# Expert rows scattered to fixed rows per token, and a final stage that reads plain rows

## The chip, the core and the metric

The kernel runs on one core of a Trainium2 chip. The metric is the device time of one execution in microseconds, as the median of several runs; lower is better. The engines are named as the profile does: PE (TensorE matmul), PEld (its weight load), DVE (VectorE), ACT (ScalarE), POOL (GpSimd) and SP (SyncE, which only issues DMAs here). A DMA queue belongs to the engine that issues: q1 is SP's, q10 ACT's, and q0 is POOL's, whose descriptors are made in software.

## The reference

One step of a one-layer decoder trunk in float32 for 1024 prompt rows and 32 sample rows, D_MODEL 1024. Token mixers (a state-space branch and a dilated attention branch) come first, then a mixture of 32 experts: each token takes one of four groups and two experts in it. The part around the change:

```
gsel  = argmax(group logits);  w_top, e_top = top_k(softmax(expert logits in the group), 2), normalised
combine[token, expert] = p_group * w_top                      # two nonzeros per token
for e in range(32):
    hid = silu(x @ w_exp_gate[e]) * (x @ w_exp_up[e])         # 1024 -> 256
    out = out + combine[:, e:e+1] * (hid @ w_exp_down[e])     # 256 -> 1024
x = x + gt2 * out                                             # adaLN gate of prompt or sample
y = x * rsqrt(mean(x*x) + 1e-6) * g_final
```

So each of the 1056 tokens has two expert rows of 1024 values. They are added to the token's residual row x2, and the sum is normalised.

## The kernel before, in words

**Stages.** The adaLN vectors and the input projection run to 310 us, then attention with the state-space inputs (to 481 us), the state-space scan, the branch projections, the merge, and from about 820 us one block of code that has the output projection, the router, the expert rounds and the final stage. Every stage is a block with one program per engine; engines meet through semaphores, and the program order within one engine is fixed by hand.

**Attention stage** (lines 880 to 910). POOL is free there but for writing a zero row of the scratch tensor `expert_rows` and the value rows of the outputs. It waits for all of them at the end of the stage.

**Routing.** Token and expert rows are placed in 23 blocks of 128 slots: each expert has 96 slots (the last but one 64), a block is `ROUNDS` index b. VectorE and TensorE work out `slot_i` (the slot of each token's first and second expert), `token_of_slot` (`tok_i`, 4096 for an empty slot) and `weight_of_slot`. Tokens that find their expert full, or that belong to the last expert, go to spare blocks (`token_of_overflow`), at least one, whose number is only known at run time; the loops `Fori(0, turns)` serve them. In the profiled execution there is one turn.

**A round** b (lines 2525 to 2605 for TensorE): POOL gathers the h2 rows of the block's tokens by an indirect DMA, which skips empty slots (line 2345); TensorE turns them (L2529, ACT copies), multiplies with the gate and up weights (L2550, four groups of 32 slots), ACT and DVE make the hidden rows, TensorE turns them (L2559) and multiplies with the down weights (L2572). In TensorE's order iteration b is gate_up(b), turn_x(b+1), down(b-1), turn_hid(b). DVE multiplies both halves of a down product with the token's gate (L3061, L3062) into one of two buffers `y_e`, and ACT stores the buffer to 128 rows of `expert_rows` in slot order (L2714). SP loads the weights of the experts ahead.

**The spare block.** POOL's `loop_block(0)` (L2361 to 2370) stands right behind its last gather; it copies the token numbers and gathers the rows. TensorE turns them (`turn_loop_x(0)`, L2605) after the last round's turn_hid and before `down(ROUNDS - 1)`. Then come gate and up (L2617), the turning (L2621), down (L2629) and the gating into `ly` (L3103).

**The final stage**, inside the loop. POOL stores the last block (L2377) and, per tile of 128 tokens, gathers the first expert's rows (L2385) and gathers the second expert's rows with an add into the same buffer `gr` (L2391). TensorE puts the spare block's rows in token order with a product by a matrix of ones and zeros (L2638), and for five tiles adds `gr` by a product with the identity (L2642). DVE adds the result to x2 (L3119, L3134), ACT squares and sums (L2739, L2741), DVE scales (L3149, L3153) and SP stores (L2324).

Of the kernel before, what the change touches and what calls it, by code (L numbers as in the profile page):

```python
# [14 lines left out]
ALU = mybir.AluOpType  # L15
# [3 lines left out]
I32 = mybir.dt.int32  # L19
# [29 lines left out]
NO_TOKEN, NO_SLOT = 4096, 8192  # L49
# [26 lines left out]
def build(nc, I, O, scratch):  # L76
    ctx = ExitStack()
    with ctx:
# [794 lines left out]
        with ExitStack() as st:  # L873
# [5 lines left out]
            zeros = sb("zero_row", [P, KT], stack=st)  # L879
            g_att = sb("gate_units_att", [P, GB, CW], stack=st)  # L880

            with nc.Block() as block:
                @block.gpsimd
                def _(pool):
# [4 lines left out]
                    pool.dma_start(scratch["expert_rows"][ROUNDS * P:ROUNDS * P + 1, :].rearrange("o (p c) -> p (o c)", p=P),  # L889
                                   zeros[:, :]).then_inc(s_vst, 16)  # L890

                    total = 0
# [17 lines left out]
                    pool.wait_ge(s_vst, 16 * (total + 1))  # L910
# [1210 lines left out]
        tok_i = sb("token_of_slot", [P, ROUNDS], I32)  # L2121
        w_slot = sb("weight_of_slot", [P, ROUNDS])
        tok_ov = sb("token_of_overflow", [P, OVB + 1], I32)
        w_ov = sb("weight_of_overflow", [P, OVB + 1])
        w_top = sb("w_top", [P, 2, NT])
        blk_i = sb("expert_of_block", [1, OVB + 1], I32)
        ids = sb("ids", [P, NT])
# [4 lines left out]
        idx = sb("idx", [P, 1], I32)  # L2132
# [101 lines left out]
        s_lfl, s_rc8 = sem("loop_first_cleared"), sem("x3_root_inverted")  # L2234
        s_lprep, s_lgs = sem("loop_tables_ready"), sem("loop_sample_rows_gated")
        s_lrp, s_lad = sem("loop_rows_of_tile_in_psum"), sem("loop_rows_added")
# [10 lines left out]
        def load_down(sp, e):  # L2247
# [4 lines left out]
        s_gf, s_first, s_both, s_mx, s_sq8, s_m8, s_rt8, s_y8, s_os8 = (  # L2252
            sem("g_final_loaded"), [sem(f"first_rows{t}_gathered") for t in range(NT)], [sem(f"second_rows{t}_added") for t in range(NT)],
            sem("x3_ready"), sem("x3_squares"), sem("x3_mean_square"), sem("x3_root"), sem("y_ready"), sem("y_stored"))
        gr = ([ring_all[:, 4096 + 1024 * t:5120 + 1024 * t] for t in range(4)] + [big[:, 12864 + 1024 * t:13888 + 1024 * t] for t in range(4)]
              + [big[:, 0:1024]])
        loop_gate, loop_at = w_gu_sb[0][:, 0:D], w_gu_sb[0][:, D:D + NT * P].rearrange("p (t n) -> p t n", t=NT)
        tile_first, loop_rel, loop_is = (sb(name, [P, NT]) for name in ("first_of_tile", "loop_token_in_tile", "loop_is_prompt"))
        ADD_ORDER = [TT] + list(range(TT))
        BY_PRODUCT = range(2, 7)  # L2260
# [3 lines left out]
        PAIR = [psum[:, i:i + 2, :] for i in (0, 2, 6, 4)]  # L2264
# [4 lines left out]
        g_row = row_p["gate1"]  # L2269
        def at_of(t):  # L2270
            return slice(TILES.index(t), TILES.index(t) + 1)


        with nc.Block() as block:
            @block.sync
# [917 lines left out]
```

## Time and profile before

| | us |
|---|---|
| median of 3 runs | 1427.6 (1423.43 to 1430.71) |
| span of the profiled execution | 1427.1 |
| own time of the profiled execution beyond its span | not given by the page |
| PE busy | 1343.0 (94%) |
| DVE / ACT / POOL busy | 606.5 / 323.6 / 118.3 |
| mean DMA rate over the span | 171 GB/s |

The span runs from the first to the last instruction of one execution. PE is busy for 94% of it, but this is an average: the last 60 us or so are the final stage, where other engines and the DMA queues work too. The page cuts the span into 40 slices; in the last two PE is busy for 7 and 6 tenths, in all slices of the rounds for 9 or more. Stretches are read from the view of busy time by window, single waits from the instructions in order of time.

### The profile page before, as it was taken

The numbers are of one execution on the slowest core, as the hardware profiler recorded it, in microseconds if no ns is written. First come the engines' busy times: TensorE is split into PE (matmuls) and PEld (weight loads), VectorE is DVE, ScalarE is ACT, GpSimd is POOL, SyncE is SP. The second block draws the span as 40 slices with busy tenths as digits, with TensorE's granted clock in tenths as the row PEclk, the third lists the DMA queues.
The fourth block names the chain that finished last, engine by engine and source line by source line (L and its number), as shares of the span: only waits on it lengthen the run. The fifth ranks groups of instructions, "written<-read, shape, count | busy, mean of one in ns | idle before, by whom it ended". The sixth has DMA issues, their size and how long they took to land. (4 is left out here: it accounts for less than half of the span.)

```text
span 1427.1 us, 21105 instructions
## 1 busy us (share of the span) xinstructions
PE 1343.0 (94%) x8689; PEld 804.0 (56%) x8689; DVE 606.5 (43%) x1290; ACT 323.6 (23%) x692; POOL 118.3 (8%) x135
## 2 busy tenths in 40 slices
PE   4899999999999899999999999999968999999976
PEld 2344448876677666666667666788863333333323
DVE  6743452324342236930752244443663532222247
ACT  4200003545443211123312122111221111110013
POOL 0000001130000060010000000000001000000042
PEclk9999999999999999999999999999968999999997
DMA  9435235330001552332313074620066999999878
GB/s 359 124 96 172 94 99 173 102 96 22 22 28 64 157 171 77 131 90 41 71 53 130 5 246 139 208 96 38 31 245 219 360 376 412 419 416 414 338 250 239
DMA packets 121473, 243.47 MB, mean 171 GB/s; under 512 B 23159, under 2 KB 87303, under 8 KB 112137
## 3 DMA queue, kind: packets, MB, share of 16 engines
q1 hardware_dynamic: 98368, 191.69, 37.7%
q10 hardware_dynamic: 14690, 28.26, 5.3%
q0 software_dynamic: 8320, 22.17, 5.1%
q8 instruction: 69, 1.13, 0.3%
q14 instruction: 26, 0.21, 0.1%
HBM read 208.30 MB, written 37.07 MB: 172 GB/s over the span
## 5 line engine op out<-in xcount | busy, mean ns | idle before, releaser
L2411 PE MATMUL psum<-ring,big 128*128 128x256 f32 x512 | 117.0, 387 | 0.0
L1308 PE MATMUL psum<-h_t,ring 128*128 128x352 f32 x368 | 111.4, 461 | 1.1 <-ACT gate_units L1599 1.1
L2411 PEld LDWEIGHTS psum<-ring,big 128*128 128x128 f32 x512 | 98.4, 195 | 13.9 <-issue 0.4
L2550 PE MATMUL psum<-w_gate_up,u_rows 128*32 128x512 f32 x608 | 101.4, 607 | 2.9 <-DMA w_gate_up<-in_w_exp_up 1.1
L2550 PE MATMUL psum<-ring,u_rows 128*32 128x512 f32 x576 | 101.4, 598 | 0.9 <-ACT u_rows L2699 0.9
L1308 PEld LDWEIGHTS psum<-h_t,ring 128*128 128x128 f32 x368 | 69.0, 190 | 38.3 <-issue 1.6
L2572 PE MATMUL psum<-big 128*32 128x512 f32 x736 | 83.7, 595 | 0.0
L469 PE MATMUL psum<-big,u_rows 128*128 128x512 f32 x144 | 63.9, 593 | 0.0
L2092 PE MATMUL psum<-big,h_t 128*128 128x352 f32 x192 | 60.5, 459 | 1.9 <-PEq L2045 1.9
L2709 ACT ACTIVATE big<-psum 128x256 f32<-128x256 f32 x23 | 8.8, 385 | 231.9 <-PE psum L2550 231.9
L3061 DVE TENSOR_SCALAR v_new<-u_rows,v_new 128x512 f32<-128x512 f32 x46 | 25.1, 546 | 81.4 <-PE psum L2572 80.6
L2550 PE MATMUL psum<-big,u_rows 128*32 128x512 f32 x288 | 56.5, 594 | 1.6 <-DMA w_gate_up<-in_w_exp_up 1.6
L523 PE MATMUL psum<-ring,u_rows 128*128 128x256 f32 x256 | 57.1, 380 | 0.0
L3046 DVE SCALAR_TENSOR_TENSOR big<-big,weight_of_slot,psum 128x256 f32<-128x256 f32 x23 | 11.1, 481 | 107.4 <-ACT big L2709 107.4
L955 PE MATMUL psum<-ring 128*128 128x512 f32 x120 | 55.5, 605 | 0.0
L2550 PEld LDWEIGHTS psum<-w_gate_up,u_rows 128*32 128x32 f32 x608 | 27.0, 112 | 48.1 <-issue 46.5
L791 DVE TENSOR_TENSOR big<-big,psum 128x512 f32<-128x512 f32 x30 | 20.6, 688 | 77.7 <-PE psum L469 77.3
L1069 ACT ACTIVATE p_sb<-s_sb,o_sb 128x128 f32<-128x128 f32 (+1 forms) x96 | 42.0, 439 | 45.4 <-DVE o_sb L1031 45.4
L523 PEld LDWEIGHTS psum<-ring,u_rows 128*128 128x128 f32 x256 | 47.9, 190 | 6.9 <-issue 0.8
L2092 PEld LDWEIGHTS psum<-big,h_t 128*128 128x128 f32 x192 | 36.4, 190 | 22.5 <-issue 2.4
L2550 PEld LDWEIGHTS psum<-ring,u_rows 128*32 128x32 f32 x576 | 26.0, 110 | 40.0 <-issue 38.9
L469 PE MATMUL psum<-h_t,ring 128*128 128x512 f32 x96 | 45.2, 615 | 2.3 <-DVE h_t L756 2.3
(542 smaller groups left out, 2164.6 us busy)
## 6 DMA issues: line engine op xcount, KB each, us to landing
big<-in_w_exp_down SPq DMA_DIRECT2D x32, 1024.0 KB, 10.7
ring<-in_w_ada SPq DMA_DIRECT2D x24, 1024.0 KB, 7.7
w_gate_up<-in_w_exp_gate SPq DMA_DIRECT2D x13, 1024.0 KB, 13.8
w_gate_up<-in_w_exp_up SPq DMA_DIRECT2D x13, 1024.0 KB, 17.1
ring<-in_w_exp_gate SPq DMA_DIRECT2D x13, 1024.0 KB, 10.9
ring<-in_w_exp_up SPq DMA_DIRECT2D x13, 1024.0 KB, 13.2
ring<-in_w_in SPq DMA_DIRECT2D x11, 1024.0 KB, 10.1
h_t<-tmp_gates SPq DMA_DIRECT2D x48, 176.0 KB, 2.6
```

What stands on the lines that cost most here:

```text
L469: m = nc.tensor.matmul(bank_of(g, x), a[:, k, :], h[:, k, :], start=(first and k == 0), stop=(last and k == 3), skip_group_check=True)
L523: m = nc.tensor.matmul(bank[e % NB][:, 0:WB], tokens, w[:, k, :], start=(k == 0), stop=(k == KT - 1))
L791: V.tensor_tensor(out, other, where, ALU.add).then_inc(s_pd, 1)
L955: m = nc.tensor.matmul(bank[7], u_tile[t % 2][:, k, :], w_[:, k], start=(k == 0), stop=(k == KT - 1))
L1069: m = A.activation(p_sb[:, i % 2, s, 0:w], s_sb[:, i % 2, s, 0:w], ACT.Exp, bias=o_sb[:, i % OB, h, HD:HD + 1], scale=1.0, accum_out=o_sb[ ...
L1308: m = T_.matmul(bank[4 + u % 4][:, 0:CW], w_[:, k, c0:c0 + P], ht3[:, k, j * CW:(j + 1) * CW], start=(k == 0), stop=(k == KT - 1))
L2092: m = T_.matmul(bank[b0 + 2][:, 0:CW], w_bs[:, k, m_ * P:(m_ + 1) * P], y2_t[:, k, tok], start=(k == 0), stop=(k == 3))
L2411: m = T_.matmul(bank[2 * (i % 2) + b // 2][0:r, (b % 2) * WB:(b % 2 + 1) * WB], merged_t[:, k, t * P:t * P + r], w[:, k, :], start=(k == 0 ...
L2550: m = T_.matmul(bank[i][at, :], x_t[i][:, k * P + CHUNK * c:k * P + CHUNK * (c + 1)], w_gu[use_of(e, GSLOTS)[0]][:, :, k, :], start=(k == ...
L2572: m = T_.matmul(down_bank(b, f)[at, :], turned(hid_t[b % 2])[:, k, at], w_dn[use_of(e, DSLOTS)[0]][:, k, f * 512:(f + 1) * 512], start=(k ...
L3046: V.scalar_tensor_tensor(out=hid[b % 2], in0=sil[b % 2], scalar=w_slot[:, b:b + 1], in1=bank[b % 2][:, FF:2 * FF], op0=ALU.mult, op1=ALU.m ...
L3061: c.step(dve, V.tensor_scalar(slot_gate, row_p["gate2"][:, at], of_prompt[:, b:b + 1], of_sample[:, b:b + 1], ALU.mult, ALU.add))
```

## The change

- The scratch tensor `expert_rows` gets 4096 rows instead of 2945: row t holds token t's first expert row, row 2048 + t its second, and 128 rows behind token 1055's second one (from 3104) take what belongs to nobody. POOL zeroes rows 0 to 1055 and 2048 to 3231 in the attention stage, by 19 DMAs.
- Every slot now knows its row (`row_of_slot`): an empty one has 6143, which the scatter skips, and the token is the row's low 11 bits.
- POOL, not ACT, writes the expert rows: an indirect scatter per round, behind gather(b) for round b-4; the scatter of round 21 stands ahead of `loop_block(0)`, that of round 22 behind it.
- The spare block's rows are added to their tokens' second rows by an indirect scatter that adds; places without a token add into the rows from 3104. The loop holds only this.
- SP loads the first rows of all tiles with three plain DMAs once all scatters have landed, and the second rows with nine once the adding scatter has landed. DVE, POOL and TensorE add them to x2, in the order FINAL.
- The mean square is taken with the scale and the added epsilon on ACT; the DVE instruction between square and root goes. DVE scales some tiles from PSUM.

The core of the diff:

```diff
-NO_TOKEN, NO_SLOT = 4096, 8192
+TOKENS = 2048
+NO_TOKEN, NO_SLOT = 3 * TOKENS - 1, 8192
+SPILL = TOKENS + N
@@ attention stage, POOL
+cleared = [(a, min(P, end - a)) for start, end in ((0, N), (TOKENS, SPILL + P)) for a in range(start, end, P)]
+for a, r in cleared:
+    pool.dma_start(scratch["expert_rows"][a:a + r, :], zeros[0:r, :]).then_inc(s_vst, 16)
@@ SP, inside the loop, behind the spare block's weight loads
+for i in range(2):
+    sp.wait_ge(s_yst[i], 16 * ((ROUNDS + 1 - i) // 2))
+for i in range(2):
+    sp.dma_start((ring_all[:, 4096:8192] if i == 0 else big[:, 12864:16960]).rearrange("p (t d) -> p t d", t=4),
+                 scratch["expert_rows"][512 * i:512 * (i + 1), :].rearrange("(t p) d -> p t d", p=P)).then_inc(s_fa[i], 16)
+sp.dma_start(gr[TT][0:NS, :], scratch["expert_rows"][SEQ:N, :]).then_inc(s_fa[2], 16)
@@ SP, behind the loop
+sp.wait_ge(s_lst, 16 * turns)
+for t in FINAL:
+    sp.dma_start(gs[t][0:r, :], scratch["expert_rows"][TOKENS + t * P:TOKENS + t * P + r, :]).then_inc(s_fb[t], 16)
+for j, t in enumerate(FINAL):
+    sp.wait_ge(s_y8, j + 1)
+    sp.dma_start(dst, gr[t][0:rows_of(t), :]).then_inc(s_os8, 16)
@@ POOL
+def scatter(b):
+    pool.wait_ge(s_dna, b + 1)
+    pool.wait_ge(s_dnd, b + 1)
+    G.indirect_dma_start(scratch["expert_rows"], bass.IndirectOffsetOnAxis(ap=row_i[:, b:b + 1], axis=0), y_e[b % 2], None,
+                         bounds_check=2 * TOKENS - 1, oob_is_err=False).then_inc(s_yst[b % 2], 16)
 gather(0)
 for b in range(1, ROUNDS):
     if b >= 2:
         pool.wait_ge(s_tx, b - 1)
     gather(b)
+    if b >= 4:
+        scatter(b - 4)
+for b in range(ROUNDS - 4, ROUNDS - 2):
+    scatter(b)
...
-    pool.wait_ge(s_lxg, 16 * (n + 1))
+scatter(ROUNDS - 2)
 loop_block(0, slice(0, 1))
-pool.dma_start(scratch["expert_rows"][P * (ROUNDS - 1):P * ROUNDS, :], y_e[(ROUNDS - 1) % 2]).then_inc(s_lst, 16)
-(18 indirect gathers, first and second rows of nine tiles)
+scatter(ROUNDS - 1)
...
 with pool.Fori(0, turns) as n:
     loop_block(n + 1, bass.ds(n + 1, 1))
+    nc.gpsimd.tensor_copy(l_row[:, :], row_ov[:, bass.ds(n, 1)]).then_inc(s_lrow, 1)
+    pool.wait_ge(s_ly, n + 1)
+    nc.gpsimd.indirect_dma_start(scratch["expert_rows"], bass.IndirectOffsetOnAxis(ap=l_row[:, 0:1], axis=0), ly, None,
+                                 compute_op=ALU.add).then_inc(s_lst, 16)
+    pool.wait_ge(s_lst, 16 * n + 16)
+for t in BY_POOL:                                     # tiles 6 and 7
+    G.tensor_tensor(x2[:, t, :], x2[:, t, :], gr[t], ALU.add).then_inc(s_x2a, 1)
+(sample rows: first rows times gate, added; second rows times gate, added: four operations on 32 partitions)
@@ PE, behind the loop
+for t in (2, 3):
+    start_sum(t, (x2[:, t, :], gr[t]))                # products with the identity into PSUM
+end_sum(2); end_sum(3)                                # the second rows
+for t in BY_POOL:
+    start_sum(t, (x2[:, t, :],))
+end_sum(6); end_sum(7)
@@ DVE
+V.tensor_scalar(tok_i[:, :], row_i[:, :], TOKENS - 1, None, ALU.bitwise_and)
+for t in BY_DVE:                                      # tiles 0, 1, 4, 5: first rows, then second rows in end_add
+    c.step(dve, V.tensor_tensor(x2[:, t, :], x2[:, t, :], gr[t], ALU.add))
@@ the order of the tiles
+FINAL = [0, 2, 1, 3, 4, 6, TT, 5, 7]
```

## Rows read from the trace of the kernel before

**Rows 1.** Stretches: busy us of PE, PEld, DVE, ACT, POOL; then clock, DMA share, GB/s.

```profile
320.00:330.00 10.00, 10.00 (x65) 7.18 (x63) 4.52 (x5) 6.85 (x19) 0.00 (x0) 1.00 0.07 22
1176.00:1200.00 24.00, 24.00 (x216) 8.15 (x212) 6.77 (x12) 2.82 (x4) 1.98 (x2) 1.00 1.02 419
1390.00:1400.00 10.00, 8.40 (x14) 3.71 (x15) 4.39 (x6) 1.35 (x3) 7.46 (x5) 0.68 1.05 286
```

**Rows 2.** What TensorE waited for from 1070 us: engine line, releaser, us, times, longest.

```profile
PE psum L2642 <- DMA ring<-tmp_expert_rows,slot_i: 7.2, 1, 7.2
...
PE psum L2550 <- DMA w_gate_up<-in_w_exp_up: 2.8, 2, 1.6
...
PE psum L2550 <- DMA ring<-in_w_exp_up: 0.6, 1, 0.6
```

**Rows 3.** Instructions of POOL in order of time: start us, us, engine, line, operation.

```profile
311.96 2.17 POOL L905 DMA_DIRECT2D out_pv<-big  x4
...
508.36 3.85 POOL L1289 TENSOR_TENSOR big<-b_bar_c,powers 128x2048 f32<-128x2048 f32 x1 [24.46 <-DVEq L1452]
```

**Rows 4.** VectorE's last instruction before the first gather, same columns.

```profile
1068.33 0.18 DVE L2962 SCALAR_TENSOR_TENSOR token_of_slot<-psum,found_so_far 128x23 int32<-128x23 f32 x1 [0.67 <-PE psum L2472]
```

**Rows 5.** Line 2345, the gathers of the rounds: ns min/median/max, and landing.

```profile
L2345 POOL DMA_INDIRECT big<-tmp_h_rows,token_of_slot x23: 989/992/1143, 1069.5 to 1320.5; - x23
...
DMA to landing us min/median/max: 4.4/8.0/9.5
```

**Rows 6.** The chain of waits in the rounds: start us, us, engine, line, count.

```profile
1077.24 9.59 PE psum L2550 x64
...
1101.35 7.00 PE psum L2550 x64
...
1113.39 7.00 PE psum L2550 x64
```

**Rows 7.** Instructions in order of time, from the spare block's gather to the last round.

```profile
1332.70 0.18 POOL L2363 COPY loop_weight<-weight_of_overflow 128x1 f32<-128x1 f32 x1 [11.21 <-PE psum L2529]
...
1334.01 1.01 POOL L2368 DMA_INDIRECT big<-tmp_h_rows,idx  x1 [0.87 <-POOL idx L2365]
...
1360.08 1.06 PE L2605 MATMUL psum<-ident,big 128*128 128x128 f32 x8
...
1361.07 3.64 PE L2572 MATMUL psum<-big 128*32 128x512 f32 x32
...
1362.50 0.69 DVE L3062 TENSOR_TENSOR big<-psum,v_new 128x512 f32<-128x512 f32 x1
...
1366.72 0.69 DVE L3062 TENSOR_TENSOR u_rows<-psum,v_new 128x512 f32<-128x512 f32 x1
```

**Rows 8.** The chain of waits, where the last round's rows are stored.

```profile
1367.99 2.94 DMA tmp_expert_rows<-u_rows
```

**Rows 9.** Instructions in order of time in the final stage.

```profile
1377.61 1.23 DVE L3103 TENSOR_TENSOR big<-psum,w_gate_up 128x1024 f32<-128x1024 f32 x1 [3.96 <-PE psum L2629]
...
1391.60 3.78 PE L2642 MATMUL psum<-ring,identity_in_first_turn 128*128 128x512 f32 x4 [7.17 <-DMA ring<-tmp_expert_rows,slot_i]
...
1420.78 1.06 ACT L2739 ACTIVATE ring<-h_t 128x1024 f32<-128x1024 f32 x1 [0.99 <-DVE h_t L3134]
...
1422.67 1.28 DVE L3153 SCALAR_TENSOR_TENSOR big<-h_t,ss,u_rows 128x1024 f32<-128x1024 f32 x1
```

**Rows 10.** Line 2391, the gathers that add: landing of its nine DMAs.

```profile
DMA to landing us min/median/max: 4.9/9.7/12.3
```

**Rows 11.** DMA queues from 1371 to 1427 us: packets, MB, share of 16 engines.

```profile
q0 software_dynamic: 2544, 8.65, 62.7%
q1 hardware_dynamic: 1200, 4.33, 19.4%
```

**Rows 12.** The same from 1080 to 1330 us.

```profile
q10 hardware_dynamic: 2609, 9.51, 9.4%
q0 software_dynamic: 3024, 7.46, 8.0%
```

More of the change, by code:

```diff
@@ L2124, in build @@
         w_ov = sb("weight_of_overflow", [P, OVB + 1])
+        row_ov = sb("row_of_overflow", [P, OVB], I32)
+        spill = sb("spill_row", [P, 1])
         w_top = sb("w_top", [P, 2, NT])
         blk_i = sb("expert_of_block", [1, OVB + 1], I32)
-        ids = sb("ids", [P, NT])
+        ids = [sb(f"ids{i}", [P, NT]) for i in range(2)]
         ss5 = sb("ss5", [P, NT])
@@ L2256, in build @@
               + [big[:, 0:1024]])
[L2257 to L2260, printed above, removed]
+        gs = ([w_gu_sb[1][:, 1024 * t:1024 * (t + 1)] for t in range(4)] + [big[:, 4160 + 1024 * t:5184 + 1024 * t] for t in range(2)]
+              + [big[:, 7232 + 1024 * t:8256 + 1024 * t] for t in range(2)] + [big[:, 1024:2048]])
@@ L2396, in _ @@
+                c.step(pool, G.tensor_tensor(gs[TT][0:NS, :], gs[TT][0:NS, :], gate_s, ALU.mult))
+                G.tensor_tensor(x2_s, x2_s, gs[TT][0:NS, :], ALU.add).then_inc(s_x3s, 1)
             @block.tensor
@@ new lines, in _, with end_add, scale @@
+                for t in BY_DVE:
+                    dve.wait_ge(s_fa[A_LOAD[t]], 16 * turns)
+                    c.step(dve, V.tensor_tensor(x2[:, t, :], x2[:, t, :], gr[t], ALU.add))
+                def end_add(j):
+                    t = FINAL[j]
+                    if t in BY_DVE:
+                        dve.wait_ge(s_fb[t], 16)
+                        V.tensor_tensor(x2[:, t, :], x2[:, t, :], gs[t], ALU.add).then_inc(s_x3d, 1)
+                def scale(j):
+                    t = FINAL[j]
+                    r = rows_of(t)
+                    src = PAIR[BY_PE.index(t)] if t in BY_PE else halves(x2_of(t)[0:r, :])
+                    dve.wait_ge(s_rt8, j + 1)
+                    V.reciprocal(ss8[0:r, t:t + 1], ss8[0:r, t:t + 1]).then_inc(s_rc8, 1)
+                    dve.wait_ge(s_rc8, j + 1)
+                    V.scalar_tensor_tensor(out=halves(gr[t][0:r, :]), in0=src, scalar=ss8[0:r, t:t + 1], in1=halves(g_row[0:r, :]),
+                                           op0=ALU.mult, op1=ALU.mult).then_inc(s_y8, 1)
@@ L3162 @@
+                dve.wait_ge(s_gf, 16)
+                for j in range(NT + 1):
+                    if j < NT:
+                        end_add(j)
+                    if j >= 1:
+                        scale(j - 1)
 _OUT = [("y_p", (1, SEQ, D)), ("y_s", (DEC_B, DEC_T, D)),
```

228 lines of the change are left out of this document (89 added, 139 removed).

## The prediction

> **What bounds the kernel now.** Read first the table of busy time by stretch: TensorE is busy throughout every stretch of the attention stage and of the expert rounds, and the DMA engines reach a share of 1.02 and 419 GB/s in the rounds [rows 1]. So a round is held by TensorE, with the transfers just behind it. The list of what TensorE waited for from 1070 us on says how close: weights that came late cost 2.8 us and, by a further row of 0.6 us that stands under it, 3.4 us over 23 rounds; the largest wait of all, 7.2 us, is for rows gathered in the final stage [rows 2]. Then the instructions in order of time around the end of the rounds [rows 7] and in the final stage [rows 9], because the change touches little else. The last round's two halves are written into y_e by 1367.41 us (the second VectorE product starts at 1366.72 and takes 0.69), and the span ends at 1427.1: 59.7 us of tail. There the queues tell what runs: the indirect gathers of q0 move 8.65 MB in 62.7% of 56 us = 35.1 us of all engines (246 GB/s), while the plain stores of q1 move 4.33 MB in 10.9 us (397 GB/s) [rows 11]. The tail is a DMA tail, dear because half of its gathers also add.
>
> **Attention stage.** 19 DMAs of zero rows (9 for rows 0 to 1055, 10 for rows 2048 to 3231) stand in POOL's queue instead of one, 9.2 MB. POOL issues four such DMAs in 2.17 us [rows 3], so 19 take 10.3 us, and its value stores start that much later. At 400 GB/s they hold the DMA engines for 23 us. Beside them TensorE works on what is in SBUF, with the DMA share at 0.07 from 320 to 330 us [rows 1]; the attention rows' stores have four buffers, one per 7 us or so. POOL next has work 160 us later. Cost 0; without that cover it would be at most the 10.3 us. Between 0 and 10.3 I take the near end, since nobody waits there.
>
> **Router.** The second table of ids, epsilon and the spill row are set on VectorE while TensorE merges: 0. The slot map gets a second dependent instruction ahead of the first gather; the existing one takes 0.18 us [rows 4]: +0.2.
>
> **Rounds.** The 22 stores that ACT issued become scatters by POOL. POOL's order is gather(b), then scatter(b-4), which waits for the halves of round b-4. With a period of 12.04 us (1101.35 to 1113.39, [rows 6]; gate and up 7.0, turning 1.1, down 3.6, [rows 6, 7]) gather(b) is issued 0.8 us after the turning of an earlier round; the down product ends 3.6 us later and the two copies 2.6 us after that, so POOL stands in the scatter until some 8 us after the turning and is back 4 us before the next gather. y_e has two buffers, and the scatter has 20 us to land. What changes is bytes: the stores of q10 move every slot and the gathers only slots that hold a token, 9.51 MB against 7.46 MB for about as many rounds [rows 12]; the scatter skips empty slots as the gather does. It costs 20 us of engines for its 7.46 MB (8.0% of 250 us) and replaces 23.5 us. That is 3.5 us off a queue that made TensorE wait 3.4 us. Bounds: -3.4 (all of that wait) and +13 (below, the second rival). I take -2.0.
>
> **The spare block's input.** This is the step that costs. In POOL's order scatter(ROUNDS-2) now stands ahead of loop_block(0), and that scatter waits for the copies of round 21. Before, loop_block(0) ran at 1332.70 and its gather was issued at 1334.01 [rows 7], under cover of two rounds. TensorE's program still turns the gathered rows *before* down(22): turning at 1360.08, down(22) at 1361.07. After: the copies of round 21 end at 1363.19 (1362.50 + 0.69), POOL starts 0.7 later (0.6 from the last copy's end at 1367.41 to the store in [rows 8], and a little for the index) and issues for 0.99 [rows 5]: 1364.9. Three small copies and the gap from 1332.70 to 1334.01 are 1.3 us, with 0.3 for the step between: the gather is issued at 1366.5. It lands after 4.4 (the least of 23, [rows 5]; the median of 8.0 belongs to a full queue; few rows are valid, so below 4.4, to 2.9, is possible as well): 1370.9. TensorE turns at 1371.0 instead of 1360.08: **+10.9**, and everything behind it, down(22), the copies, the spare block's products, goes with it. This wait is new; queued behind it are down(22), the last scatter and both stages of loads.
>
> **The clock.** TensorE has then stood for 9 to 10 us. After a gap of 7.2 us at 1391.60 four products took 3.78 us, and the stretch of 1390 to 1400 has a mean granted clock of 0.68 [rows 9, 1], the two levels being 1.2 and 2.4 GHz. Round 0, after a wait, needs 9.59 for the 64 products that take 7.00 in another round [rows 6]: 2.6. A turning of 1.06 at half speed costs 1.1 more: 3.7. The first turning may count toward what the products need, so I take **+3.0**, bounds 0 and 3.7. By the Trainium skill, "TensorE: Matmul & The Clock Gate", section "Loop structure matters more than you think", a DMA wait of 8 us drops the clock; the trace agrees with its 7.2 us.
>
> **The final stage.** Copies of round 22 end at 1367.4 + 13.9 = 1381.3. The scatter starts 0.6 later; a plain store of the same size landed 2.94 us after issue [rows 8], and I add 1 us for the indirect form: 1385.9. SP then loads the first rows of all tiles, 4.33 MB at 397 GB/s = 10.9 us, landed by 1399. The spare rows are gated at 1378.84 + 13.9 = 1392.7 (the product of 1377.61 lasts 1.23, [rows 9]). POOL's adding scatter starts at 1393.4; a gather that adds landed after 4.9 to 12.3, median 9.7 [rows 10]. Its 0.5 MB goes beside the first loads; I take 7.5, so it has landed at **S = 1400.9**. Only then may SP load the second rows: the first tile's are there at S + 3, the last's at S + 14. The adding of the first rows on VectorE, POOL and TensorE is done beside the waiting. From S + 3: one add 1.23, a square 1.06 [rows 9] with read-out, root and gaps 0.9: the first scaling starts at S + 6.2. Behind it VectorE has nine scalings with their reciprocals at 1.5 (1.28 for the scaling, [rows 9], the rest a guess for the small one) and three more adds at 1.25: S + 23.5. POOL's way is shorter: two adds of 128x1024 at half of the 3.85 of a 128x2048 [rows 3], and four operations on the sample rows at the same 1.93, two of them after their second rows (S + 11.5): S + 15.4, then ACT and VectorE for three tiles: S + 21. The DMA way: second rows until S + 14, stores of 4.33 MB beside the scaling, 10.9 us: S + 25, no later than the last store. For leaving the loop and for VectorE and POOL on each other's feet I add 1: S + 24.5. From the last scaling's end (1422.67 + 1.28) to the span's end it is 3.15 now, and again: S + 27.7 = 1428.5.
>
> The second-rows gathers with their adding, 24 us of engines (35.1 less 10.9), and the products by the placing matrices go; what is late next is the adding scatter, then VectorE.
>
> **Sum** in the profiled execution: rounds -2.0, map +0.2, input and clock +13.9, tail from the end of the copies 47.2 (1428.5 less 1381.3) instead of 59.7, so -12.5; together -0.4: 1426.7. The page gives no time beyond the span of 1427.1, which lies 0.5 under the median 1427.6 of runs from 1423.43 to 1430.71. Adding 0.5: **1427**.
>
> One rule speaks against it. The row of 3.85 us shows POOL's adding with VectorE nearly idle beside it. By the Trainium skill, "SBUF — State Buffer", section "SBUF: two separate sides", a VectorE operation with two SBUF inputs and a GpSimd operation that reads SBUF exclude each other, the later one waiting for all of the earlier. No row of before shows that meeting; it is a rival below.
>
> **Rivals.**
> *The tail is shorter than drawn* (0.25). The adding scatter lands after 4.9 instead of 7.5 (-2.6), the spare rows' gather after 2.9 instead of 4.4 (-1.5), the late weights vanish (-1.4), the clock costs 1 less, 1.5 of VectorE's gaps close: -8, **1419**. For it: few valid rows. Against it: the adding scatter writes all 128 rows, beside full loads.
> *POOL's queue makes gathers late* (0.13, the other side). The gather must land before the next turning, 12.04 - 1.1 - 0.8 = 10.1 us after issue; it lands after 8.0, at most 9.5 [rows 5]. If the scatter ahead of it on the same queue adds over 2.1 us, each of 19 rounds waits for the excess: at 2.8 us 0.7 x 19 = 13, **1440**. Against it: both together are 0.7 MB per round.
> *VectorE and POOL block each other at the end* (0.08): four POOL operations of 1.93 = 7.7 us lie in VectorE's chain: +7, **1434**.
> *The stall is not there* (0.06): TensorE finds the spare rows in time, -13.9, **1413**. The order in POOL's and TensorE's programs speaks against it.
> The forecast has 0.48; its own range is 1421 to 1434. All together, 1415 to 1440. A measurement of this kernel can tell some 0.5% (7 us) from no change, so faster means under 1420.5: 0.30 (two rivals, a little less for the part of the first that stays inside); same 0.49; slower 0.21 (the second rival, most of the third, the forecast's own edge).
>
> **What would show it.** A wait of TensorE of 9 to 11 us before the line that turns the spare block's rows, released by a DMA from the h2 rows; a clock under 1.00 in the 10 us behind it; round periods of 12.04 with waits for weights under 3.4 us in all; 25 to 30 us from the landing of the adding scatter to the end; q0 no longer at 246 GB/s. The forecast is wrong if the wait is under 5 us, if the rounds' gathers are waited for, or if the end follows the adding scatter by over 33 us.

## The result, and the profile after

| | before | after |
|---|---|---|
| median | 1427.54 us (20 runs, 1421.19 to 1434.2) | 1431.69 us (20 runs, 1426.86 to 1440.31) |
| ratio | | 1.0031, 95% interval 1.0016 to 1.0046 |
| span of the profiled execution | 1427.1 | 1429.4 |
| copies of the last round's rows end, to the span's end | 59.7 | 52.5 |

The changed kernel is slower by 0.3%, which 20 runs of each tell from zero. The forecast was 1427 us, no change: the measured median lies 4.7 us above it, inside the forecast's own range of 1421 to 1434, and no slowdown was forecast. The stretches of the two profiled executions say where the difference is. They are cut at instructions that both kernels have: POOL's first zeroing, POOL's first instructions in the next stage and in the router, the first gather, TensorE's start on the last round's turn_hid, and the span's end.

| us | attention | scan to merge | router | rounds | tail |
|---|---|---|---|---|---|
| before | 171.60 | 338.85 | 249.14 | 290.33 | 67.29 |
| after | 173.25 | 338.42 | 245.96 | 288.05 | 72.39 |

The first three columns vary alike in kernels with and without the change: over the fourteen profiled executions of this study (the two kernels and the twelve experiments) attention takes 171.6, 173.25 or 174.7 to 174.9, scan to merge 338.4 to 341.5, the router 245.8 to 246.0, 249.1 to 249.4 or 251.05. The stretch ahead of the table varies as well, from 308.8 to 311.3 (1.4 of the 2.3 us between the two spans lie there). So what the change did is in the last two columns: the rounds gave back 2.3 us and the tail took 5.1. "Tail" is from here on the last column.

**The rounds.** The queues from 1080 to 1330 us of the changed kernel (packets, MB, share of 16 engines), against [rows 12]:

```profile
q1 hardware_dynamic: 14023, 79.13, 79.5%
q0 software_dynamic: 5690, 14.43, 15.1%
```

q10, on which ACT stored 9.51 MB, is no longer in the list, and q0 went from 7.46 to 14.43 MB: 7.0 MB written in place of 9.5.

What TensorE waited for from 1070 us on (engine line, releaser, us, times, longest), against [rows 2]:

```profile
PE psum L2639 <- DMA big<-tmp_h_rows,idx: 13.9, 2, 10.6
PE psum L2563 <- DMA big<-tmp_h_rows,token_of_slot: 3.4, 1, 3.4
PE psum L2677 <- DMA w_gate_up<-tmp_expert_rows: 2.5, 2, 1.9
...
PE psum L2584 <- DMA w_gate_up<-in_w_exp_up: 1.5, 1, 1.5
```

Late weights cost 1.5 us instead of 3.4. The one wait of 3.4 for a round's gather is that of the first round, 3.6 before. At the head of the list is a wait that the kernel before did not have, 10.6 us for the rows of the spare block. (The second of its two times, 3.4 us, is at 1390.38, for the gather of the next spare block, which holds nothing; TensorE then stands again for 1.9 us before the second rows are there, so this one is covered.)

**The spare block's input.** Instructions of POOL and of TensorE in order of time; each line is start us, us, engine, line, operation, and in brackets the idle time before it with its releaser:

```profile
1361.24 0.97 POOL L2377 DMA_INDIRECT tmp_expert_rows<-big,row_of_slot  x1 [10.51 <-DVE big L3111]
...
1363.55 1.06 POOL L2400 DMA_INDIRECT big<-tmp_h_rows,idx  x1 [0.90 <-POOL idx L2397]
```

```profile
1368.01 1.94 PE L2639 MATMUL psum<-ident,big 128*128 128x128 f32 x8 [10.56 <-DMA big<-tmp_h_rows,idx]
1369.88 4.26 PE L2606 MATMUL psum<-big 128*32 128x512 f32 x32
```

POOL issues the scatter of round 21 only when VectorE has written that round's rows, and the gather stands behind it. The gather lands 4.3 us after its issue, and by then TensorE has stood for 10.56 us. Then the turning takes 1.94 instead of 1.06 and the down product 4.26 instead of 3.64 [rows 7]. The stretch of 1368 to 1378 us has a mean granted clock of 0.84 (columns as in [rows 1]):

```profile
1368.00:1378.00 10.00, 9.99 (x49) 4.36 (x50) 2.48 (x4) 1.02 (x1) 0.30 (x1) 0.84 0.17 54
```

**The final stage.** VectorE from the first tile's second rows on, in order of time, and then POOL in the same stretch (L3157 adds the second rows, L3166 scales; L2422 is the adding of tiles 6 and 7, L2425 to L2429 are the four operations on the sample rows):

```profile
1400.79 2.42 DVE L3157 TENSOR_TENSOR h_t<-h_t,w_gate_up 128x1024 f32<-128x1024 f32 x1 [3.76 <-DMA w_gate_up<-tmp_expert_rows]
1404.74 0.16 DVE L3164 RECIPROCAL ss<-ss 128x1 f32<-128x1 f32 x1 [1.54 <-ACT ss L2788]
1404.94 1.55 DVE L3166 SCALAR_TENSOR_TENSOR ring<-h_t,ss,u_rows 128x1024 f32<-128x1024 f32 x1
1406.42 3.36 DVE L3157 TENSOR_TENSOR h_t<-h_t,w_gate_up 128x1024 f32<-128x1024 f32 x1
1409.70 0.15 DVE L3164 RECIPROCAL ss<-ss 128x1 f32<-128x1 f32 x1
1409.88 1.28 DVE L3166 SCALAR_TENSOR_TENSOR ring<-psum,ss,u_rows 128x1024 f32<-128x1024 f32 x1
...
1413.00 3.35 DVE L3157 TENSOR_TENSOR h_t<-h_t,big 128x1024 f32<-128x1024 f32 x1
...
1420.69 1.22 DVE L3157 TENSOR_TENSOR h_t<-h_t,big 128x1024 f32<-128x1024 f32 x1
...
1425.04 1.28 DVE L3166 SCALAR_TENSOR_TENSOR big<-psum,ss,u_rows 128x1024 f32<-128x1024 f32 x1
```

```profile
1389.08 2.62 POOL L2416 DMA_INDIRECT tmp_expert_rows<-big,loop_row  x1 [4.17 <-DVE big L3147]
1397.48 4.64 POOL L2422 TENSOR_TENSOR h_t<-h_t,big 128x1024 f32<-128x1024 f32 x2 [5.78 <-DMA tmp_expert_rows<-big,loop_row]
1402.08 3.32 POOL L2425 TENSOR_TENSOR big<-big 32x1024 f32<-32x1024 f32 x1
1405.48 3.21 POOL L2426 TENSOR_TENSOR big<-big 32x1024 f32<-32x1024 f32 x1
1408.77 3.22 POOL L2428 TENSOR_TENSOR big<-big 32x1024 f32<-32x1024 f32 x1
1412.07 3.20 POOL L2429 TENSOR_TENSOR big<-big 32x1024 f32<-32x1024 f32 x1
```

Four adds of one shape, on one line of the program: 2.42, 3.36, 3.35 and 1.22 us. The three long ones lie beside POOL's operations, which end at 1415.27; the last, at 1420.69, has none beside it. The scaling at 1409.88 also lies beside a POOL operation and takes its 1.28: its wide input is in PSUM. That at 1404.94 has both wide inputs in SBUF and takes 1.55.

The ends of the rows say more. POOL's operations end at 1402.12, 1405.40, 1408.69, 1411.99 and 1415.27. VectorE's add of 1400.79 ends at 1403.21, its scaling of 1404.94 at 1406.49, its adds of 1406.42 and 1413.00 at 1409.78 and 1416.35: each 1.1 us behind a POOL operation's end, which is about what such an instruction needs by itself. And POOL's next operation, on its way already, ends 2.2 us behind that VectorE instruction (1403.21 to 1405.40, 1406.49 to 1408.69, 1409.78 to 1411.99). This is how it looks when two engines take turns, a whole instruction each: the 3.2 of a POOL row would be 1.0 of waiting and 2.2 of its own. The split is worked out from these ends; no row shows an operation on 32 partitions with VectorE idle. The durations on POOL are the rougher ones in a profile, so the reading is tested below by e2 and e11 on VectorE's rows and on the end.

The adding scatter was issued at 1389.08 and landed 8.0 us later: S, the moment of its landing as in the prediction, is 1397.1. From S to the end it is 32.3 us, where 27.7 were forecast. The figure repeats: in e1, e5, e6 and e7 below, which have the same final stage, it is 32.3 in each, and 32.8 in e8.

### The profile page after: what moved, and what is told of

It is laid out like the page before. It is cut to its first block and busy times, and to the rows that moved or that the text cites. A ratio compares the mean times of both kernels' runs of the same rounds, so it can differ in the third digit from the quotient of the medians.

```text
span 1429.4 us, 21068 instructions
## 1 busy us (share of the span) xinstructions
PE 1335.9 (93%) x8673; PEld 800.3 (56%) x8673; DVE 603.9 (42%) x1272; ACT 323.0 (23%) x691; POOL 149.0 (10%) x165
## 5 line engine op out<-in xcount | busy, mean ns | idle before, releaser
L2445 PE MATMUL psum<-ring,big 128*128 128x256 f32 x512 | 114.0, 380 | 0.0
```

What stands on the lines that cost most here:

```text
L2445: m = T_.matmul(bank[2 * (i % 2) + b // 2][0:r, (b % 2) * WB:(b % 2 + 1) * WB], merged_t[:, k, t * P:t * P + r], w[:, k, :], start=(k == 0 ...
```

## Experiments

The theory after the comparison has three terms: the input gather's place costs the tail some 12 us, the meeting of VectorE and POOL 4 to 5 us, and the plain final stage gives back more than it seemed to. The rival: the end follows the DMAs (the adding scatter and the loads), and VectorE's long adds are a symptom. The ratio is always to the kernel before on the same chip; for the changed kernel it is 1.0031 (1.0016 to 1.0046). In the code, `...` marks what is left out.

### e1: the spare block's input early

```diff
-for b in range(ROUNDS - 4, ROUNDS - 2):
-    scatter(b)
+scatter(ROUNDS - 4)
...
-scatter(ROUNDS - 2)
 loop_block(0, slice(0, 1))
+scatter(ROUNDS - 3)
+scatter(ROUNDS - 2)
```

> The changed kernel, with the spare block's row gather issued ahead of the scatters of rounds 20 and 21 instead of behind them. Theory: the wait of TensorE ahead of the turning of these rows (10.6 us in the changed kernel's trace) and the half-speed work behind it (1.94 for 1.06 us of turning, 4.2 for 3.6 us of down product, 1.5 us together) go: 12 us less, some 1417.5 us of span against 1429.4, ratio to the kernel before about 0.993. Rival (the tail is held by transfers: whatever comes earlier only waits longer for the loads): under 4 us less, 1425 or more.

Measured: 1418.92 us, ratio 0.9933 (0.9908 to 0.9959), tail 60.45 against 72.39. TensorE in the same place, without a wait:

```profile
1358.62 1.06 PE L2639 MATMUL psum<-ident,big 128*128 128x128 f32 x8
1359.61 3.64 PE L2606 MATMUL psum<-big 128*32 128x512 f32 x32
```

The place of one gather, ahead of two scatters or behind them, is worth 11.9 us of tail, and with the gather ahead the changed kernel is faster than the one before.

### e2: POOL's adds on VectorE

```diff
 # POOL: the adds of tiles 6 and 7 and the four operations on the sample rows go ...
+for t in BY_POOL:                                   # DVE, before end_add
+    V.tensor_tensor(x2[:, t, :], x2[:, t, :], gr[t], ALU.add).then_inc(s_x2a, 1)
...
+c.step(dve, V.tensor_tensor(gr[TT][0:NS, :], gr[TT][0:NS, :], gate_s, ALU.mult))
+c.step(dve, V.tensor_tensor(x2_s, x2_s, gr[TT][0:NS, :], ALU.add))
 # DVE, in end_add, for the sample rows
...
+    c.step(dve, V.tensor_tensor(gs[TT][0:NS, :], gs[TT][0:NS, :], gate_s, ALU.mult))
+    V.tensor_tensor(x2_s, x2_s, gs[TT][0:NS, :], ALU.add).then_inc(s_x3s, 1)
```

> The changed kernel, with the six additions and products of POOL in the final stage (two tiles' first rows, four on the sample rows) moved to VectorE. Theory (the two engines exclude each other): VectorE's additions of 128x1024 fall from 2.4 to 3.4 us back to 1.23 and the adding of the second rows is 4 to 6 us shorter, less 2.5 us for the two sample operations that VectorE now has there: 2 to 4 us less, ratio to the changed kernel 0.997 to 0.9985. Rival (VectorE is slow there because of the loads writing to SBUF): its additions stay at 2.4 to 3.4 us and the time rises by 4 us or more.

Measured: 1430.49 us, ratio 1.0015 (0.9997 to 1.0033), tail 70.52. The line of the adds (durations ns min/median/max):

```profile
L3158 DVE TENSOR_TENSOR h_t<-h_t,w_gate_up x2: 1221/1223/1225, 1403.8 to 1407.9; 128x1024 f32<-128x1024 f32 x2
L3158 DVE TENSOR_TENSOR h_t<-h_t,big x2: 1215/1216/1217, 1412.1 to 1420.0; 128x1024 f32<-128x1024 f32 x2
```

All four are back at 1.22. The adding scatter, issued at 1390.3, landed after 8.5, so S to the end is 29.9, 2.4 less than in the changed kernel, although VectorE now does six more operations; the two that fall behind the first add of second rows hold its chain for 2.4. That VectorE ended sooner with more work is what the rival of the DMAs can't give: the loads are the same. In the median the gain of 2 us is too small to tell, and the interval overlaps that of the changed kernel.

### e3: both

> Both edits: the spare block's gather early and the additions on VectorE. Theory: they add up, 14 to 16 us less than the changed kernel, span 1413 to 1416, ratio to the kernel before 0.990 to 0.992. Rival (transfers hold the tail once the stall is gone): no better than the early gather alone, 1417 or more.

The edits of e1 and e2 together. Measured: 1415.86 us, ratio 0.9919 (0.9895 to 0.9944), tail 57.89. S to the end is 29.9 again (issued at 1375.7, landed after 6.5, span 1412.1), against 32.3 in e1. The two gains add: 11.9 and 1.9 us of tail alone, 14.5 together. With both losses undone the tail is 9.4 us under that of the kernel before, 57.89 against 67.29: this is what the plain final stage gives back, the third term. What its parts give (plain loads for gathers, the shorter way on ACT, scaling from PSUM) was not run apart.

### e4: the kernel before, its input late

```diff
+pool.wait_ge(s_dna, ROUNDS - 1)
+pool.wait_ge(s_dnd, ROUNDS - 1)
 loop_block(0, slice(0, 1))
```

> The kernel before, with one thing of the change alone: POOL waits for both halves of round 21's rows before it issues the spare block's gather. Theory: TensorE waits for the gather as in the changed kernel, some 9 us, and its clock falls: 10 to 12 us more, ratio 1.007 to 1.0085. Rival (the old tail is a DMA tail that would swallow part of it): 5 us more or less, since the gathers of the final stage wait for the last round's rows in either case and only these are late: their start shifts in full, so anything under 8 us speaks for the rival.

Measured: 1439.69 us, ratio 1.0086 (1.0061 to 1.0111), tail 77.09 against 67.29: +9.8. TensorE's wait, and the two instructions behind it:

```profile
1371.03 1.94 PE L2607 MATMUL psum<-ident,big 128*128 128x128 f32 x8 [8.58 <-DMA big<-tmp_h_rows,idx]
1372.91 4.34 PE L2574 MATMUL psum<-big 128*32 128x512 f32 x32
```

The wait and the clock (0.88 + 0.70 = 1.6) appear in the old kernel from this one edit. The wait is 2 us shorter: no scatter stands ahead of the gather, which is issued 4.8 us after the start of the last turn_hid instead of 6.5 and lands in 4.1 instead of 4.3. 8.6 + 1.6 = 10.2 for the 9.8 of the tail. With e1 this term is shown from both sides.

### e5: products in the wait

```diff
 pe.wait_ge(s_txc, ROUNDS)
+for _ in range(11):
+    T_.matmul(bank[1], ident[:, :], row_p["gate2"][:, 0:512], start=True, stop=True)
 turn_loop_x(0)
```

> The changed kernel, with eleven products of 128x512 that nobody reads put on TensorE into the wait for the spare block's rows (9.5 us of work in a wait of 10.6). Theory: the wait stays and only the clock is kept; the turning of the rows takes 1.06 again for 1.94 us and the down product 3.6 for 4.2, so 1.5 us less than the changed kernel, ratio to the kernel before 1.002. Rival (the clock costs the 3 us of the prediction, since the spare block's products are slowed as well): 3 us less, 1.001. Rival (the products push the down product back): the same time or more.

Measured: 1431.64 us, ratio 1.0016 (0.9997 to 1.0034), tail 71.11. TensorE in the wait and behind it:

```profile
1361.66 9.61 PE L2644 MATMUL psum<-u_rows,ident 128*128 128x512 f32 x22
1372.24 1.16 PE L2639 MATMUL psum<-ident,big 128*128 128x128 f32 x8 [0.97 <-DMA big<-tmp_h_rows,idx]
1373.33 3.64 PE L2606 MATMUL psum<-big 128*32 128x512 f32 x32
...
1386.17 5.37 PE L2665 MATMUL psum<-big 128*128 128x512 f32 x8 [0.71 <-DVE big L3146]
```

With TensorE kept busy the turning takes 1.16 and the down product 3.64: 1.4 us of the stall are the clock, the rest is the wait, and the tail is 1.3 shorter. But the spare block's down product, 3.67 in the changed kernel, is 5.37 here (granted clock 0.66 from 1386 to 1391), and so it is in e1, e3 and e12, though not in e9 (3.67, granted clock 1.00). It makes the adding scatter 1.7 us later and costs the tail next to nothing: the scatter is issued 9.8 us after the first rows' loads instead of 8.1, and lands after 6.6 instead of 8.0.

### e6: plain stores of all slots in the rounds

```diff
-    G.indirect_dma_start(scratch["expert_rows"], bass.IndirectOffsetOnAxis(ap=row_i[:, b:b + 1], axis=0), y_e[b % 2], None,
-                         bounds_check=2 * TOKENS - 1, oob_is_err=False).then_inc(s_yst[b % 2], 16)
+    pool.dma_start(scratch["expert_rows"][P * b:P * (b + 1), :], y_e[b % 2]).then_inc(s_yst[b % 2], 16)
```

> The changed kernel, with POOL's scatter of a round replaced by a plain store of all 128 slots to 128 rows in slot order, from the same place in POOL's program; the rows that the final stage then reads are other tokens' rows. Theory (the rounds are 2 to 2.5 us shorter because empty slots are not written): the rounds take 2 to 2.5 us more than in the changed kernel, from the first gather to the last turning of the hidden rows 290 to 290.5 us against 288.05. Rival (they are shorter because ACT no longer issues or the queue is another): they stay at 288.

Measured: 1435.2 us, ratio 1.0038 (1.0017 to 1.0058), tail 72.40, rounds 290.19 against 288.05 of the changed kernel and 290.33 of the one before. The queue and TensorE's waits:

```profile
q0 software_dynamic: 5616, 16.90, 17.2%
```

```profile
PE psum L2583 <- DMA w_gate_up<-in_w_exp_up: 2.8, 2, 1.5
...
PE psum L2583 <- DMA ring<-in_w_exp_up: 0.6, 1, 0.6
```

POOL issues from the same places, only the bytes are those of before, and the 3.4 us of late weights are back. In the eleven kernels that scatter the rows, the changed one among them, the rounds take 287.3 to 288.3. So the rounds' gain is bytes, as expected; in the medians (1.0038 against 1.0031) it does not show.

### e7: 32 zeroing DMAs instead of 19

```diff
-for start, end in ((0, N), (TOKENS, SPILL + P))
+for start, end in ((0, 2 * TOKENS),)
```

> The changed kernel, with all 4096 rows zeroed in the attention stage, 32 DMAs and 16.8 MB instead of 19 and 9.2 MB. Theory (the zeroing costs nothing, it lies beside a stage whose DMA share is 0.07): the same time as the changed kernel within 1 us, and the attention stage ends at the same time. Rival (the zeroing costs up to the 10.3 us that POOL needs to issue it, in part): 2 to 7 us more.

Measured: 1431.54 us, ratio 1.0022 (1.0004 to 1.0041). POOL in the changed kernel, and here:

```profile
312.58 9.93 POOL L893 DMA_DIRECT2D tmp_expert_rows<-zero_rows  x19 [0.30 <-POOL zero_rows L889]
```

```profile
311.46 16.73 POOL L893 DMA_DIRECT2D tmp_expert_rows<-zero_rows  x32 [0.30 <-POOL zero_rows L889]
```

Thirteen more cost 6.8 us of POOL and the median doesn't move. The attention stage took 174.73 in this execution, but 174.94 in e4 too, with the old zeroing; and with the new zeroing it took 171.6, as in the kernel before, in e1, e3, e6, e8 and e9. A kernel that zeroes nothing was not tried, as the final stage would read rows that nobody wrote.

### e8: the scatter of the spare block without its add

> The changed kernel, with the spare block's scatter writing instead of adding, so that the second rows of its tokens hold only the spare block's part. Theory (the adding scatter takes 8.0 us to land because each row is read, added and written, behind the first rows' loads): it lands after 4 to 5 us, 3 to 4 us less in all. Rival (it takes so long because it shares the engines with 4.3 MB of loads, whatever it does): it still lands after 7 us or more and the time stays.

```diff
-...ly, None, compute_op=ALU.add).then_inc(s_lst, 16)
+...ly, None).then_inc(s_lst, 16)
```

Measured: 1428.66 us, ratio 1.0004 (0.9984 to 1.0024), tail 72.36. The scatter landed after 7.4 instead of 8.0: the expected 4 to 5 were missed, and the rival held. The adding isn't what makes it take so long. The interval overlaps that of the changed kernel, and the tail is the same.

### e10: the first rows loaded behind the adding scatter

```diff
 # SP: moved from inside the loop to behind s_lst, ahead of the second rows
...
+for i in range(2):
+    sp.dma_start(..., scratch["expert_rows"][512 * i:512 * (i + 1), :]...).then_inc(s_fa[i], 16)
+sp.dma_start(gr[TT][0:NS, :], scratch["expert_rows"][SEQ:N, :]).then_inc(s_fa[2], 16)
```

> The changed kernel, with SP's loads of the first rows held back until the adding scatter has landed. Theory (the scatter's 8.0 us are mostly the sharing of the engines with 4.3 MB of loads): it lands after 4 to 5 us. The whole is 7 to 9 us slower than the changed kernel, since the second rows come 10.9 us later and 3.5 are won: ratio to the kernel before 1.008 to 1.009. Rival (its own read, add and write set the time): it still takes 7 us or more to land, and the whole is over 10 us slower.

Measured: 1449.2 us, ratio 1.0134 (1.0107 to 1.0161), tail 86.53: +14.1, more than was expected. With nothing beside it the scatter landed after 6.3: in the changed kernel's 8.0 about 6 us are its own and 1.7 the company of the loads, so neither account of the landing holds whole. All traces together say more. In the eleven kernels that load the first rows early, the scatter was issued 8.1 to 9.9 us after these loads and landed 15.9 to 16.6 us after them (15.5 without its add, e8), and the later it was issued, the sooner it landed: 7.7 to 8.5 us after its issue for the five that add and were issued 8.1 to 8.2 behind the loads, 6.4 to 6.6 for the four at 9.8 to 9.9. So in these kernels S follows the first rows' loads; 1.7 us earlier or later in the issue hardly moves it. What the loads' early place is worth is more than their 10.9 us. VectorE in order of time:

```profile
1409.74 2.48 DVE L3149 TENSOR_TENSOR h_t<-h_t,ring 128x1024 f32<-128x1024 f32 x2 [15.12 <-DMA ring<-tmp_expert_rows]
1415.22 6.69 DVE L3149 TENSOR_TENSOR h_t<-h_t,big 128x1024 f32<-128x1024 f32 x2 [2.99 <-DMA big<-tmp_expert_rows]
1421.94 3.25 DVE L3155 TENSOR_TENSOR h_t<-h_t,w_gate_up 128x1024 f32<-128x1024 f32 x1
```

The adds of the first rows now come after the wait, and two of them, beside POOL's adds from 1415.20 on, take 6.69 instead of 2.48.

### e11: no operations on the sample rows

```diff
-c.step(pool, G.tensor_tensor(gr[TT][0:NS, :], gr[TT][0:NS, :], gate_s, ALU.mult))
-c.step(pool, G.tensor_tensor(x2_s, x2_s, gr[TT][0:NS, :], ALU.add))
...
-c.step(pool, G.tensor_tensor(gs[TT][0:NS, :], gs[TT][0:NS, :], gate_s, ALU.mult))
-G.tensor_tensor(x2_s, x2_s, gs[TT][0:NS, :], ALU.add).then_inc(s_x3s, 1)
+pool.sem_inc(s_x3s, 1)
```

> The changed kernel, without the four operations of POOL on the 32 sample rows (their expert rows are left out of the sum), the two on tiles 6 and 7 kept. Theory (each of the two engines' operations waits for the other's): VectorE's additions behind the first take 1.22 instead of 3.36 us, and from the landing of the adding scatter to the end it is 27.5 to 28.5 us instead of 32.3, so 4 to 5 us less than the changed kernel, ratio to the kernel before 0.9995 to 1.0005. Rival (the additions are slow for another reason, such as loads that write at the same time): they stay above 2.4 us and under 1 us is won.

Measured: 1424.54 us, ratio 0.9966 (0.9947 to 0.9985), tail 68.01. The line of the adds:

```profile
L3154 DVE TENSOR_TENSOR h_t<-h_t,w_gate_up x2: 1218/1636/2055, 1405.9 to 1410.9; 128x1024 f32<-128x1024 f32 x2
L3154 DVE TENSOR_TENSOR h_t<-h_t,big x2: 1214/1216/1219, 1415.0 to 1420.6; 128x1024 f32<-128x1024 f32 x2
```

Without the four small operations on 32 partitions, three adds take 1.22 and one, beside POOL's add of tile 7, 2.06. The scatter landed at 1393.7 + 8.1, so S to the end is 27.5: 4.8 under the changed kernel, near the 27.7 of the forecast. VectorE's work is unchanged here, and the four operations of POOL are left out: 4.8 is their price. The add that still meets POOL waits 0.84 us, which is in the 27.5. The medians differ by more (0.9966 against 1.0031, some 9 us; the intervals leave 4 and up), of which the traces show only the 4.4 of the tail.

### e9 and e12: the adds of tiles 6 and 7 on TensorE

Both are e3 with the first rows of tiles 6 and 7 added by products with the identity. In e9 these stand ahead of the sums of tiles 2 and 3, in e12 behind them:

```diff
 # e9
-end_sum(2)
-end_sum(3)
+pe.wait_ge(s_fa[1], 16 * turns)
 for t in BY_POOL:
...
-    pe.wait_ge(s_x2a, BY_POOL.index(t) + 1)
-    start_sum(t, (x2[:, t, :],))
+    start_sum(t, (x2[:, t, :], gr[t]))
+end_sum(2)
+end_sum(3)
 # e12, behind end_sum(2) and end_sum(3)
+pe.wait_ge(s_fa[1], 16 * turns)
 for t in BY_POOL:
...
-    pe.wait_ge(s_x2a, BY_POOL.index(t) + 1)
-    start_sum(t, (x2[:, t, :],))
-end_sum(6)
-end_sum(7)
+    start_sum(t, (x2[:, t, :], gr[t]))
+    end_sum(t)
```

> Both edits of the third experiment, and the first rows of tiles 6 and 7 added by TensorE (products with the identity, before the second rows come) instead of VectorE. Theory (in the third experiment VectorE was 1.1 us late for the first tile's second rows because of these two additions): 1 to 2 us less than it, span about 1411 for rounds of the same length, ratio to the kernel before 0.990 to 0.992, and from the landing of the adding scatter to the end 28.5 us instead of 29.8. Rival (VectorE's chain starts when the second rows land, whatever it did before): the same as the third.

Measured: 1415.29 us, ratio 0.9901 (0.9882 to 0.9921), but the tail is 60.21, longer than e3's 57.89. S (1373.6 + 7.7) to the end is 32.7, where 28.5 was expected. TensorE in order of time, and what VectorE waited for:

```profile
1389.46 1.88 PE L2662 MATMUL psum<-big,ident 128*128 128x512 f32 x4
1391.17 3.60 PE L2667 MATMUL psum<-w_gate_up,ident 128*128 128x512 f32 x8
```

```profile
DVE ss L3163 <- ACT ss L2778: 6.0, 4, 4.1
```

Tile 2 was in TensorE's queue behind adds that nobody wanted yet, and VectorE stood 4.1 us for it.

> The kernel of e3 (input early, the adds of tiles 6 and 7 and of the sample rows on VectorE), but TensorE adds the first rows of tiles 6 and 7 itself: eight more products, placed behind the two sums of tiles 2 and 3, each tile finished before the next begins. In e9 the same products stood ahead of the sums of tiles 2 and 3 and held them back to 1391.17; here nothing stands ahead of them. In e3 TensorE began the second part of the sums at 1387.39 and 1393.58, each group of eight at full speed 3.60 us, and VectorE scaled tile 6 from 1402.19 and tile 7 from 1407.74. Here tile 6 is ready at 1393.6 + 3.6 + 1.8 = 1399.0 and tile 7 at 1399.0 + 3.6 + 1.8 = 1404.4, both before VectorE, 2.4 us ahead of its places, wants them. Theory (VectorE's own chain is the bound of the end): two adds of 1.22 leave it, 28 us from the landing of the adding scatter to the end in place of 29.8, span -2.4 against e3, ratio to before near 0.990. Rival (the second rows' loads, or ACT's squares and TensorE, now set the pace): the chain has other waits in the place of the two adds, 29 to 31 us, ratio 0.992 as e3. A further rival (adding at half speed): TensorE's granted clock stays at the lower level, the sums take 7 us a tile, tile 7 is ready at 1410 and the end is 3 to 5 us later than in e3, ratio 0.995.

Measured: 1417.86 us, ratio 0.9904 (0.9881 to 0.9928), tail 56.76, the shortest of all. S (1382.2 + 6.4) to the end is 28.8, against 29.9 in e3: -1.1, where -2.4 was expected. Of the two adds that VectorE was spared, only a part counted:

```profile
1392.50 1.22 DVE L3155 TENSOR_TENSOR h_t<-h_t,w_gate_up 128x1024 f32<-128x1024 f32 x1 [1.36 <-DMA w_gate_up<-tmp_expert_rows]
```

Here it waits 1.36 for the second rows of the first tile; in e3 the two adds of tiles 6 and 7 (2.36) stood there, so 1.36 of them were hidden. The theory named the right chain and overlooked that its head was covered. Against the kernel before, e3, e9 and e12 are all faster by about 1%; among the three the intervals decide nothing.

## Why the prediction was wrong, step by step

- **Attention stage and router, 0 and +0.2.** Held: e7 shows that even 6.8 us more of POOL cost nothing that can be told. The 0.2 is below what can be seen.
- **Rounds, -2.0.** Held: -2.3, and e6 shows the cause that was given, the bytes.
- **The spare block's input, +10.9.** Held: a wait of 10.56, gone in e1, made in e4.
- **The clock, +3.0.** The mechanism held. Its size in the profiled execution was half: 0.88 + 0.62 = 1.5, and in e5, with the clock kept up, 1.4 of it goes. But the size varies from one execution to the next: over the eight that have the wait (8.6 to 10.6 us) the turning takes 1.94 or 1.95 each time and the down product 4.26, 4.33, 4.34, 4.59, 4.74, 4.93, 5.03 and 5.75, a loss of 1.5 to 3.0 us, 1.9 in the middle. The 3.0 is the upper end. The 3.7 came from round 0, which needs 2.6 more for its 64 products [rows 6]; the 32 here lost 0.6 to 2.1. Input and clock together: +12.2 from the start of the last turn_hid to the end of the last down product (17.1 against 4.9), forecast +13.9.
- **The adding scatter, S.** Held: forecast 8.2 us after the spare rows are gated, measured 8.8. The 7.5 for the landing lay between 6.3 with nothing beside it (e10) and 8.0 with the loads. What sets it was not seen: S comes some 16 us after the first rows' loads, for which the forecast had 15 (1385.9 to 1400.9).
- **From S to the end, 27.7: the step that failed.** "For leaving the loop and for VectorE and POOL on each other's feet I add 1". It was 32.3: above the 25 to 30 that the prediction named as its sign, under the 33 that would have refuted it. e11 takes POOL's small operations away and leaves VectorE's: 27.5, and 26.7 without the 0.84 that one add still waits. The forecast without its allowance of 1 was 26.7 as well, so in place of the allowance stood 5.6 us, 4.8 of them from the four small operations. (That the rest agrees so well is in part luck: in e11 the first scaling starts at S + 7.85 instead of S + 6.2, and from there to the last scaling's end it is 16.55 instead of 17.3.) Two prices were wrong in it. VectorE's add beside a POOL operation was left at 1.25 and takes up to 3.36, as it waits for what is left of POOL's. And POOL's operation on 32 partitions was set at 1.93, half of the 3.85 of [rows 3], and has 2.2 of its own and 1.0 of waiting. The same view of the kernel before had a nearer row. The 3.85 is a product of two inputs read as broadcasts; the sum of two plain tiles, two rows on, takes 4.53, and half of it is 2.27:

```profile
516.21 4.53 POOL L1291 TENSOR_TENSOR big<-big 128x2048 f32<-128x2048 f32 x1
```

By these terms: -2.3 + 12.2 for the rounds and the stall, and the final stage from the end of the copies 52.5 less the 59.7 of before, -7.2 instead of -12.5: +2.7, the 2.8 of the rounds' and the tail's columns. The medians give 4.15, with an interval of 2.3 to 6.6. That the forecast came within 5 us owes something to chance: 1.7 us too much loss in input and clock stood against 5.3 too much gain in the final stage.

The rival of the two engines that block each other had 0.08 and +7. It was the right mechanism at two thirds of its size, and its sign was decided by it: without it the sum is -2. The rule quoted there (the Trainium skill, "SBUF — State Buffer", section "SBUF: two separate sides") is borne out: the adds and the scalings with both wide inputs in SBUF end 1.1 us behind the POOL operation that they met, and the scaling with its wide input in PSUM is not held. The chance was too small for a rule with no row against it and four POOL operations planned straight across VectorE's busiest stretch. The trace of before even had a row beside the rule, of a copy and so not of two inputs: at 518.82 us, beside the 4.53 above, VectorE copies 128x64 values from SBUF to SBUF in 1.97 us and ends with POOL's operation (at 520.79 and 520.74), where the same line takes 0.20 and 0.18 the two other times. *POOL's queue makes gathers late* fell: the only waited-for gather is the first, as before. *The tail is shorter* fell with the landing of 8.0; of its parts the cheaper clock came in the profiled execution. *No stall* fell.

What stays open: the 1.65 us steps of the attention stage and those of the router are in every kernel and were not looked into; the landing of the adding scatter was read once per kernel (6.3 to 8.5 us), so its parts are estimates, and why it follows the loads is not shown, as no run loads less ahead of it; where the second stretch at half speed falls (e1, e3, e5, e12), and why the loss behind the wait ranges from 1.5 to 3.0, is seen, not explained. The 9 us between the medians of e11 and the changed kernel, of which the traces show 4.4, are open too.

## What to carry to other kernels

When work is put into one engine's queue, look at everything that stands *behind* it there: a scatter ahead of a small gather turned a hidden load into the largest wait of these stages, and moving the gather up gave 12 us back. Spreading adds over a second engine was no gain here, where both work from SBUF: six operations that POOL took over held VectorE's chain longer, by the traces, than the same six on VectorE itself (32.3 against 29.9 us from S to the end, in two pairs of kernels; the medians can't tell it). A sum that comes to zero from +14 and -14 is a forecast of no change only if each of its terms is known to a few us; here the meeting of two engines, priced at 1 us, decided the sign, and undoing the one large loss was worth more than the whole change.

## What the runs showed of the hardware

- A VectorE add of 128x1024 with both inputs in SBUF takes 1.22 us alone and up to 3.36 beside a POOL operation. By the ends of the rows it does its work only after that one's end, and the next POOL operation only after its own. So POOL's rows read 3.2 us where 2.2 are work, and VectorE's 3.36 where 1.1 are. Few partitions don't make a POOL operation short: 2.2 us for 32x1024 (worked out from the ends), and at most 2.32 for 128x1024 (4.64 for two).
- Waits of TensorE of 8.6 to 10.6 us cost 1.5 to 3.0 us of clock in the 40 instructions behind them (1.94 for 1.06, and 4.26 to 5.75 for 3.64, over eight executions). Covering the wait with useless products took 1.4 of it away there, a later product ran at the lower clock instead (5.37 for 3.67), and the median gained nothing that can be told.
- A scatter of 512 KB that adds into DRAM landed 6.3 us after its issue with nothing beside it, and 6.4 to 8.5 beside 4.33 MB of loads issued 8.1 to 9.9 us ahead of it, always 15.9 to 16.6 us after these loads; without the add it landed after 7.4 instead of 8.0.
